# HGRN level scores: one exponential of prefix sums, formed by matmul for each level, in place of decays multiplied up on the vector engine

## The reference, cut to what matters

```python
def hgrn2_mixer(q, f_logit, i, g, lb, gn_g):
    sig = jax.nn.sigmoid(f_logit)
    log_f = jnp.log(lb + (1.0 - lb) * sig)
    key = (1.0 - lb) * (1.0 - sig)
    ...
    b = jnp.cumsum(lc, axis=3)                       # within a chunk
    ...
    pair_decay = jnp.exp(jnp.where(causal[:, :, None], diff, 0.0))   # diff = b_t - b_s
    scores = jnp.einsum('bhnck,bhnsk,bhncsk->bhncs', qc, kc, pair_decay)
    ...                                              # and a scan over chunks with exp(b_end)
    return o.reshape(bsz, seq, MIX_WIDTH) * gn_g * jax.nn.silu(g)
```

## Time and profile before

| | |
|---|---|
| time before, median of 3 runs | 2066.12 us (2063.51 to 2068.38) |
| the profiled execution | 2063.51 us, of which the span is 2061.7 us |
| TensorE busy | 1856.7 us (90%) |
| VectorE busy | 756.9 us (37%) |
| ScalarE busy | 515.8 us (25%) |
| mean granted TensorE clock | 0.958 of full |

### The profile page before, as it was taken

One profiled execution on the slowest core, in us unless ns is written; L12 is line 12 of the kernel. 1 busy time (PEld: TensorE's weight loads), 2 busy tenths in 40 slices (PEclk: granted clock), 3 DMA queues, 4 the chain that ended last, 5 costly groups with the idle time before them and its releaser, 6 DMA issues.

```text
span 2061.7 us, 25853 instructions
## 1 busy us (share of the span) xinstructions
PE 1856.7 (90%) x11206; PEld 1417.8 (69%) x11206; DVE 756.9 (37%) x1250; ACT 515.8 (25%) x782; POOL 0.2 (0%) x4
## 2 busy tenths in 40 slices
PE   8999999999999999999999999998999876566655
PEld 7899867899998898677999997456788421111111
DVE  4533333466534523334566655323444200000001
ACT  2201122344332001211544463423532210000001
POOL 0000000000000000000000000000000000000000
PEclk9999999999999999999999999999999998878788
DMA  7231333554432223537554421301126999999997
GB/s 292 82 123 62 127 159 140 207 204 164 164 143 102 69 95 139 230 121 273 205 181 177 154 80 50 137 1 41 41 82 252 424 426 427 427 427 427 428 427 307
DMA packets 30930, 413.53 MB, mean 201 GB/s; under 512 B 3424, under 2 KB 3680, under 8 KB 4320
## 3 DMA queue, kind: packets, MB, share of 16 engines
q1 hardware_dynamic: 30384, 409.32, 49.7%
q10 hardware_dynamic: 432, 2.56, 0.3%
HBM read 410.82 MB, written 1.05 MB: 200 GB/s over the span
## 4 chain that ended last, share of the span: by engine, by line
PE 76%; DMA 14%; DVE 5%; another core or an unknown queue 2%; ACT 2%; issue 1%; SPq 0%; DVEq 0%; ACTq 0%
PE ps L212 56%; PE ps L752 7%; PE ps L1499 5%; PE ps L1129 3%; DMA high<-in_w_e_down_dram 2%; DMA ring<-in_w_e_down_dram 2%; DMA high<-in_w_e_up_dram 2%; DMA ring<-in_w_e_gate_dram 2%; DMA low<-in_w_e_gate_dram 2%; DVE high L171 2%; PE ps L1162 1%; DMA ring<-in_w_in_dram 1%; ACT high L206 1%; PE ps L748 1%; DVE high L181 1%
## 5 line engine op out<-in xcount | busy, mean ns | idle before, releaser
L212 PE MATMUL ps<-high,ring 128*128 128x256 f32 (+1 forms) x2016 | 476.7, 387 | 7.6 <-DMA ring<-in_w_in_dram 5.0
L212 PE MATMUL ps<-rarena 128*128 128x256 f32 (+1 forms) x3648 | 453.3, 287 | 1.2 <-DVE low L181 0.6
L212 PEld LDWEIGHTS ps<-rarena 128*128 128x128 f32 x3648 | 445.2, 192 | 8.2 <-DVE low L181 1.0
L212 PEld LDWEIGHTS ps<-high,ring 128*128 128x128 f32 x2016 | 373.2, 190 | 76.5 <-issue 19.6
L206 ACT ACTIVATE high<-ps 128x256 f32<-128x256 f32 (+2 forms) x194 | 93.5, 482 | 651.4 <-PE ps L212 236.5
L206 ACT ACTIVATE rarena<-ring 128x2048 fp32r<-128x2048 f32 x76 | 140.0, 1842 | 258.1 <-PE ps L212 196.6
L171 DVE TENSOR_TENSOR rarena<-ring,rarena 128x2048 fp32r<-128x2048 f32 x76 | 167.3, 2201 | 97.8 <-ACT rarena L206 96.7
L171 DVE TENSOR_TENSOR high<-high,ps 128x512 f32<-128x512 f32 x52 | 35.7, 687 | 305.4 <-PE ps L1499 247.6
L752 PE MATMUL ps<-high 128*128 128x128 f32 (+6 forms) x1024 | 129.0, 298 | 9.6 <-ACT high L206 4.6
L752 PEld LDWEIGHTS ps<-high 128*128 128x128 f32 (+2 forms) x1024 | 111.5, 191 | 34.9 <-issue 13.5
L1499 PE MATMUL ps<-high,low 128*32 128x512 f32 x592 | 87.2, 716 | 52.0 <-DMA high<-in_w_e_up_dram 35.4
(11 more groups left out here) (160 smaller groups left out, 1505.4 us busy)
## 6 DMA issues: line engine op xcount, KB each, us to landing
ring<-in_w_in_dram SPq DMA_DIRECT2D x34, 2048.0 KB, 7.6
ring<-in_w_ffn_up_dram SPq DMA_DIRECT2D x22, 2048.0 KB, 7.5
high<-in_w_e_up_dram SPq DMA_DIRECT2D x20, 2048.0 KB, 49.9
high<-in_w_e_gate_dram SPq DMA_DIRECT2D x17, 2048.0 KB, 46.6
high<-in_w_e_down_dram SPq DMA_DIRECT2D x17, 2048.0 KB, 50.6
ring<-in_w_mod_dram SPq DMA_DIRECT2D x12, 2048.0 KB, 9.5
ring<-in_w_e_down_dram SPq DMA_DIRECT2D x10, 2048.0 KB, 49.0
ring<-in_w_ffn_down_dram SPq DMA_DIRECT2D x8, 2048.0 KB, 7.4
```

Source lines behind the costliest of these rows:

```text
L212: ins = self.e.matmul(out, l, r, start=first and i == 0, stop=end and i == n - 1)
```

## The change

The sum of log f over a stretch of positions is a product of the transposed log f with a matrix of zeros and ones. The new kernel

- adds nine constant 128 x 128 masks, `hw`, to the table inside `early` (and drops an unused allocation of the same size);
- takes the logarithm of `H.lf` on ScalarE in the RWKV stage (a step of `rwkv`'s generator, before the last ones);
- turns it (four transposes on TensorE into one bank, one copy on VectorE into `H.lfT`) just ahead of RWKV's last step: on TensorE between its last two empty steps and the wait for `yn`, on VectorE ahead of the `normed` that makes `yn`;
- for each level makes the sums of all positions by four matmuls of 128 rows and 128 columns (`sums_of`, one bank `he`), level 0 in round 0 and level `lev+1` at the start of the round of level `lev`; ScalarE takes the exponential into one of two buffers `H.E`, one round after; VectorE multiplies the lower halves by `H.key` and the upper halves by `B.hq`;
- the level matmul then has the same block of `H.E` as both operands;
- the three multiplications per level of before and the working copy `H.qd` are gone; in the vector program `placed(lev-1)` now stands ahead of the multiplications for level `lev`, in the same round as before.

```diff
+    hw = []
+    for i in range(7):
+        m = 1 << i
+        ref = (f // (2 * m)) * 2 * m + m - 1
+        hw.append(one(((f // m) % 2 == 1) & (p > ref) & (p <= f)) + one(((f // m) % 2 == 0) & (p > f) & (p <= ref)))
+    hw.append(one(p > f))
+    hw.append(one(p <= f))
...
-        H.qd = alloc(2, 256)
+        H.lfT = alloc(2, 256)
+        H.E = alloc(2, 2, 256)
@@ TensorE, rwkv, last steps
                 yield
                 yield
+                PE.wait_ge(f"{l}lf")
+                b = take("m", f"{l}lfT.ps", f"{l}lfT")
+                transposes([(v2(b)[:, t, 128 * i:128 * i + 128], H.lf[:, i, 128 * t:128 * t + 128])
+                            for t in range(2) for i in range(2)]).then_inc(*PE(f"{l}lfT.ps"))
                 PE.wait_ge(f"{l}yn")
@@ TensorE, hgrn
+                PE.wait_ge(f"{l}lfT")
+                def sums_of(lev):
+                    b = take("m", f"{l}he{lev}.ps", f"{l}he{lev}")
+                    for i in range(2):
+                        for t in range(2):
+                            ins = one(itn(b)[:, i, t, :], H.lfT[:, t, 128 * i:128 * i + 128],
+                                      c("hw", lev + (t if lev == 7 else 0)))
+                    ins.then_inc(*PE(f"{l}he{lev}.ps"))
+                sums_of(0)
                 yield
                 for lev in range(8):
+                    if lev < 7:
+                        sums_of(lev + 1)
+                    Eb = H.E[:, lev % 2, :, :]
                     bs = [take("m", f"{l}hl{lev}{n}.ps", f"{l}hl{lev}{n}") for n in range(2)]
                     PE.wait_ge(f"{l}hE{lev}")
                     if lev < 7:
                         for hd, t in hchunks:
                             po, n = 64 * (hd % 2), at_(hd, t)
-                            ins = one(bs[n // 4][:, 128 * (n % 4):128 * (n % 4) + 128],
-                                      H.key[po:po + 64, hd // 2, 128 * t:128 * t + 128],
-                                      H.qd[po:po + 64, hd // 2, 128 * t:128 * t + 128])
+                            blk = Eb[po:po + 64, hd // 2, 128 * t:128 * t + 128]
+                            ins = one(bs[n // 4][:, 128 * (n % 4):128 * (n % 4) + 128], blk, blk)
@@ ScalarE, rwkv
-                yield from none(4 + 1 + 24 + 6)
+                yield from none(4 + 1 + 24)
+                A.wait_ge(f"{l}key")
+                A.act(H.lf, H.lf, Ln).then_inc(*A(f"{l}lf"))
+                yield from none(6)
@@ ScalarE, hgrn
-                yield from none(9)
+                yield
+                for lev in range(8):
+                    A.wait_ge(f"{l}he{lev}.ps")
+                    if lev > 1:
+                        A.wait_ge(f"{l}hl{lev - 2}.ps")
+                    A.act(H.E[:, lev % 2, :, :], v2(ps(f"{l}he{lev}.ps")), Exp).then_inc(*A(f"{l}he{lev}"))
+                    yield
@@ VectorE, rwkv
+                V.wait_ge(f"{l}lfT.ps")
+                V.cp(H.lfT, v2(ps(f"{l}lfT.ps"))).then_inc(*V(f"{l}lfT"))
                 normed(f"{l}y", R.y, R.st)
@@ VectorE, hgrn
-                yield
-                for lev in range(1, 8):
...
-                    V.wait_ge(f"{l}hl{lev - 1}.ps")
-                    V.tt(part(H.qd, 1), part(H.qd, 1), total(0).to_broadcast([128, 256 // m, m]), mul).then_inc(*V())
-                    V.tt(part(H.key, 0), part(H.key, 0), total(1).to_broadcast([128, 256 // m, m]), mul).then_inc(
-                        *V(f"{l}hE{lev}"))
-                    if lev < 7:
-                        V.tt(total(1), total(1), total(0), mul).then_inc(*V())
-                    placed(lev - 1)
+                for lev in range(8):
+                    if lev:
+                        placed(lev - 1)
+                    Eb = H.E[:, lev % 2, :, :]
+                    m = 1 << lev
+                    V.wait_ge(f"{l}he{lev}")
+                    for src, half in ((H.key, 0), (B.hq, 1)):
+                        v = lambda z: flat(z).rearrange("p (b k m) -> p b k m", k=2, m=m)[:, :, half, :]
+                        V.tt(v(Eb), v(Eb), v(src), mul).then_inc(*V())
+                    V.mark(f"{l}hE{lev}")
                     yield
```

More of the change, by code:

```diff
@@ L52, in constants @@
     parts["we"] = wc - one(p == f)
+    hw = []
[5 more added lines that the diff above has]
+    hw.append(one(p <= f))
+    parts["hw"] = np.concatenate(hw, 1)
     parts["nm"] = np.concatenate([-lt, -one(p >= 0), -lt], 1)
@@ L111 @@
 CST_GROUPS = [["ident", "ones", "misc", "ge", "rmask"],
-              ["blk", "gt", "lev", "levt", "wc", "we", "nm", "negsb", "negmo", "mcos", "msin", "mrot"],
+              ["blk", "gt", "lev", "levt", "wc", "we", "hw", "nm", "negsb", "negmo", "mcos", "msin", "mrot"],
               ["acos", "asin", "arot", "flip", "bd", "e16"]]
@@ L370, in build @@
         v2r = early[:, n1 + 1600:n1 + 1856]
-        alloc(9 * 128)
         lb = alloc(L, 2)
@@ L1031, in hgrn @@
                             po, i = 64 * (hd % 2), hd // 2
-                            ins = one(bs[hd % 2][:, 128 * i:128 * i + 128], H.key[po:po + 64, i, 0:128],
-                                      H.qd[po:po + 64, i, 128:256])
+                            ins = one(bs[hd % 2][:, 128 * i:128 * i + 128], Eb[po:po + 64, i, 0:128],
+                                      Eb[po:po + 64, i, 128:256])
                     ins.then_inc(*PE(f"{l}hl{lev}.ps"))
@@ L2249, in placed @@
                                 *V(f"{l}hl{lev}{n}"))
-                yield
-                for lev in range(1, 8):
-                    m = 1 << (lev - 1)
-                    part = lambda z, half: flat(z).rearrange("p (b k m) -> p b k m", k=2, m=m)[:, :, half, :]
-                    total = lambda half: part(H.lf, half)[:, :, m - 1:m]
-                    V.wait_ge(f"{l}hl{lev - 1}.ps")
-                    V.tt(part(H.qd, 1), part(H.qd, 1), total(0).to_broadcast([128, 256 // m, m]), mul).then_inc(*V())
-                    V.tt(part(H.key, 0), part(H.key, 0), total(1).to_broadcast([128, 256 // m, m]), mul).then_inc(
-                        *V(f"{l}hE{lev}"))
-                    if lev < 7:
-                        V.tt(total(1), total(1), total(0), mul).then_inc(*V())
-                    placed(lev - 1)
+                for lev in range(8):
[8 more added lines that the diff above has]
+                    V.mark(f"{l}hE{lev}")
                     yield
@@ L2452, in forget_gates @@
                     V.mark(f"{l}key")
-                    V.wait_ge(f"{l}hq1.out")
-                    V.tt(H.qd, B.hq, H.lf, mul).then_inc(*V(f"{l}hE0"))
                     yield from none(16)
```

## The result

The changed kernel is slower. Its median is 2093.53 us of 4 runs (2089.45 to 2096.89), against 2067.25 us of 4 runs of the kernel before (2063.51 to 2073.38): the ratio is 1.0124, 95% interval 1.01 to 1.0146, or 26 us. The forecast was 21.4 us more, 2087.5. The record lists 22 runs of the changed kernel in all; their median is 2093.0 (2087.3 to 2102.8). The profiled execution has a span of 2086.4 us where the one of before had 2061.7: 24.7 more.

A forecast was written before the change was run, and what follows sets the result against it. TensorE was taken to bound the kernel, so added work costs its duration unless it fills a wait. Sums 14.2, turning 4.2, waits 1.9 and 1.1 made 21.4 us on the median 2066.1: 2087.5, range 2079 to 2095.

The forecast's parts named there:

- The sums: TensorE, mixing stages: 16 groups of four matmuls at 0.89 us, 14.2 us; bounds 0.44 each (7.0) and 1.05 each (16.8).
- The turning: Before `yT` in each layer: transposes, copy and `normed` in a chain start `yT` 2.1 us later, 4.2 us in all.
- The waits: TensorE at the mixing levels: 5.7 us against 3.8 in layer 0 (+1.9), 3.4 against 1.4 in layer 1 (+2.0).
- The wait at the transposes behind round 5: Layer 0: TensorE's 1.52 us wait for VectorE at the transposes at 285.92 goes.
- The bank of the sums: Risk: the bank not free when TensorE comes, adding up to 0.9 us in each of rounds 2 to 7.
- Costed at nothing: Larger `early` load at the start, up to 4.2 us if uncovered; logarithm's two table loads on ScalarE, at most 1 us per layer.
- The sum: Whole kernel: 14.2 + 4.2 + 1.9 + 1.1 = 21.4 us more.
- the clock falls in a new wait: Rival, chance 0.14: one to four clock falls at waits of rounds 1, 5, 8 add 1.3 to 5.2 us, 2089 to 2093.
- the likeliest case: Whole kernel: sums at full price with the waits as worked out, 2087.5 us, chance 0.60.
- Shorter chains: Rival, chance 0.13: waits in mixing shrink to the old ones, 3 us less, perhaps another 3.3 at `yn`; 2081 to 2084.5.
- Short sums: Rival, chance 0.05: the 16 groups take 0.44 us each, 7.0 for 14.2, so 2080.
- The tail as a cover: Rival, chance 0.04: transfers set the start of the expert weight stream, so the whole delay vanishes, 2066.

The follow-up runs named there:

- the kernel with the second filler step: Changed kernel with one filler step per layer moved from the mixing stage's end to ahead of round 8; 2085.01 us, ratio 1.009 to the kernel before.
- both comparisons: Changed kernel against the kernel before, measured twice: 2093.53 us, ratio 1.0124, then again without edit, 2089.98 us, ratio 1.0113.

## Why the prediction was right, and where it was short

**What bounds the kernel** held. TensorE's added work costs its full duration; 1.6 us taken from VectorE bought nothing.

**The sums** were taken at 0.89 us each, 14.2. Doubling them added another 0.89 per group at round 1 and 9.6 us over the two layers net of the waits they filled. The bounds of 0.44 and 1.05 are out.

**The turning** was put at 4.2 us; the profile shows 2.2 per layer, and moving it ahead by one step took out the 1.6 of wait and left the transposes.

**The waits** were put at 5.7 and 3.4 us; 5.9 and 3.4 came, at the levels named and with the causes named: VectorE late from `mr` in round 1, an eviction ahead of the exponential in rounds 5 and 8. Putting the exponentials ahead moved those waits back to the copies. The wait at the transposes behind round 5 went as forecast, and the weights' wait of layer 1 took 1.1 us of the sums. The bank of the sums, which the prediction had named as a risk, was never waited for: every wait at L760 in the mixing stages ends with VectorE's multiplications.

**Costed at nothing**: the start came 0.3 us later, within what it varies by itself; the logarithm's table loads, ahead of it and behind it, hid. ScalarE's timeline in the RWKV stage of after:

```profile
170.68 1.28 ACT L214 ACT_TABLE_LOAD   x1
171.97 0.63 ACT L214 ACTIVATE high<-high 128x512 f32<-128x512 f32 x1
172.68 1.28 ACT L214 ACT_TABLE_LOAD   x1
175.46 0.39 ACT L214 ACTIVATE low<-ps 128x256 f32<-128x256 f32 x1 [1.50 <-PE ps L220]
```

ScalarE is idle again behind them, waiting for TensorE. The page counts 50 loads where the earlier trace rows has 46: these two in each layer, and none for the 16 exponentials that stand among evictions with Tanh. The Trainium skill, page "ScalarE: Activation LUTs", section "Table sets: the hidden batching unit", puts Exp and Tanh in one set; the trace now agrees, which no row of before could show.

**The sum** of 21.4 us was the right size for what it covers. Without the clock's share the three profiles of after leave 20.9, 20.2 and 21.3 at the expert loads. Part of this closeness is luck: counted from the first RWKV matmul, 22.1 to 22.6 had come up by the end of layer 1's mixing, 0.7 to 1.2 more than forecast, and the feed-forward network of layer 1 gave 1.4 back, which the prediction had as unchanged. What makes the measured delay larger is the clock, as far as the profiles show it. What was missing is the first rival, *the clock falls in a new wait*, which I held for an alternative with a chance of 0.14 and which came on top of the likeliest case. Of the places it named, round 8 is the one: the clock fell behind its wait in 6 of 10 passages where the wait is 1.95 or 2.52 us, and in none of 16 where it is at most 1.17. Among the 16 are the four passages of the kernel with the second filler step. Its edit also puts more work of TensorE ahead of the wait, so no run tells the shorter wait from the longer work in front of it. A fall costs 1.7 us, more than the 1.3 I had read off one filler step, since the next groups run slow too. Two passages at 6 in 10 make 2.0 us per execution: with the 20.2 to 21.3 above that is 22.2 to 23.3, which stands within the interval of both comparisons (1.0 to 1.46% or 20.7 to 30.2 us, and 0.95 to 1.31% or 19.6 to 27.1 us). The waits of rounds 1 (1.15) and 5 (1.63), which I had named too, showed no fall.

The Trainium skill, page "TensorE: Matmul & The Clock Gate", section "Part 1: The HAM clock gate (the "warmup" mystery)", makes the low clock the default that activity lifts. The falls behind waits agree; the fall at 788 (the 12.07 us above) stands where TensorE waited for nothing.

**What stays open.** The last 3 us or so, up to the 26 us of the first comparison. In the three profiles of either kernel the loads begin 26.5 us later on average, and 5.7 of that are the clock's: 2.3 for four falls behind round 8, 2.8 for the one long fall and 0.6 for the other places. Only the first of these is tied to the change. Falls at 190 and at 770 to 790, in the matmuls of 64 columns of the RWKV stage, come in profiles of both kernels, and so do those behind the weights' waits of layer 1. The long fall between 1410 and 1460, some 8.5 us, came in 4 of 13 profiles, in one of three of after and in none of three of before, too few to say whether the change has a part in it. With a spread of 7 us and more in either kernel, the medians do not place these 3 us.

**The other rivals.** Shorter chains: no, the chains were as read. Short sums: no. The tail as a cover: no, the expert loads begin 24.3 us later and the end lies 24.7 later.

## What to carry to other kernels

Where one engine is busy nine tenths of a stage, work moved to it costs its duration and work taken from the others is worth only the waits they caused; look for the form of the same idea that leaves that engine alone, here a scan on the vector engine in place of matmuls with masks. Waits that come with such a change could be forecast here to about a tenth of a microsecond by walking each queue in its strict order, and moving one step of a generator took out the one at `yT`. Such an edit has to be judged by the whole stage: the second filler step shortened the wait in round 8 of layer 0 by 1.35 us, and the stage by 0.2. A new wait of some 2 us on TensorE amid short matmuls should be counted with what the clock may take behind it, as an addition to the forecast and not as an alternative to it.

## What the runs showed of the hardware that I had not expected

- The clock's falls are a matter of chance at one and the same place: the same program with the same wait of 2.52 us in round 8 of layer 0 fell in two of the changed kernel's three profiles, and so did its wait of 1.95 us in layer 1; only one profile had both.
- The clock also falls with no wait in front: at 190 or at 770 to 790, in 8 of the 13 profiles and in those of both kernels, in and behind matmuls of 64 columns (24 of them took 3.77 us for the usual 2.79), 1.7 us each time.
- In the second model, at the same work and with no wait, the clock was at 0.50 in 1410 to 1415 and 1420 to 1425 in one execution and at 1.00 in another, and a matmul of 128x512 took 2.07 us in place of 1.13. With some 8.5 us such a fall is the largest single difference between two profiles of one kernel.
- The table that was loaded for the logarithm did not serve what came behind it: each logarithm brought two loads of 1.28 us, one on either side.
